# Half of four units' low parts on GpSimd, and fifteen top-k rounds of block 2 ahead of attention

## What is computed

```
def dsa_sparse_attention(h, pos, w_in, w_out):
    proj = h @ w_in                       # h is the normed x: rmsnorm(x, g)
    q, k, v, qi, ki, wi = jnp.split(proj, B_SPLITS, axis=-1)
    q, k, qi, ki = (partial_rope(t) for t in (q, k, qi, ki))
    def block(args):                      # 128 queries
        logits = jnp.einsum('bthd,bsd->bths', qi_blk, ki)
        score = jnp.einsum('bths,bth->bts', jax.nn.relu(logits), wi_blk)
        score = jnp.where(key_pos <= t, score, -jnp.inf)
        _, idx = lax.top_k(score, 128)
        s = einsum(q_blk, k[idx]) * HEAD_DIM ** -0.5
        pr = jax.nn.softmax(where(idx <= t, s, -inf))
        return einsum(pr, v[idx])
    return concat(blocks) @ w_out
```

## Time and profile before

| what | value |
|---|---|
| median of 3 runs | 1077.5 us (1077.49 to 1078.8) |
| profiled execution, its own time | 1078.13 us |
| its span | 1076.3 us, mean granted clock 0.997 |
| busy | TensorE 1056.6 us (98%), weight loads 859.0, VectorE 747.4 (69%), ScalarE 538.3 (50%), GpSimd 192.7 (18%) |
| DMA | 99.94 MB, mean 93 GB/s |

### The profile page before, as it was taken

One profiled execution on the slowest core, in us unless ns is written; L12 is line 12 of the kernel. 1 busy time (PEld: TensorE's weight loads), 2 busy tenths in 40 slices (PEclk: granted clock), 3 DMA queues, 4 the chain that ended last, 5 costly groups with the idle time before them and its releaser, 6 DMA issues.

```text
span 1076.3 us, 14866 instructions
## 1 busy us (share of the span) xinstructions
PE 1056.6 (98%) x5408; PEld 859.0 (80%) x5408; DVE 747.4 (69%) x1284; ACT 538.3 (50%) x1016; POOL 192.7 (18%) x335
## 2 busy tenths in 40 slices
PE   9999999999999999999999999999999999999997
PEld 8777779888888888888778766679888888888885
DVE  5455536586697697687579898526596696696684
ACT  6677545353453443425554567645254444453422
POOL 0465320000000000005403387520000000000005
PEclk9999999999999999999999999999999999999999
DMA  9531505645545445332623333006553535535502
GB/s 294 121 79 40 118 1 119 135 88 109 101 95 118 97 99 118 90 68 51 135 43 79 79 79 79 1 1 140 116 111 85 118 81 116 117 79 118 110 9 78
DMA packets 52009, 99.94 MB, mean 93 GB/s; under 512 B 4704, under 2 KB 4832, under 8 KB 51936
## 3 DMA queue, kind: packets, MB, share of 16 engines
q1 hardware_dynamic: 51216, 98.61, 40.9%
q10 hardware_dynamic: 720, 0.38, 0.1%
HBM read 96.88 MB, written 2.10 MB: 92 GB/s over the span
## 4 chain that ended last, share of the span: by engine, by line
PE 88%; DVE 5%; DMA 3%; ACT 1%; issue 1%; SPq 1%; POOL 0%; POOLq 0%; DVEq 0%; ACTq 0%
PE bank L2038 11%; PE bank L2039 11%; PE bank L2037 11%; PE bank L2397 7%; PE bank L2398 7%; PE bank L2396 7%; PE bank L2047 6%; PE bank L2049 5%; PE bank L2048 5%; PE bank L2186 3%; PE bank L2421 3%; PE bank L2420 3%; PE bank L2422 3%; PE bank L2255 2%; DMA w_raw<-in_a_w_in 2%; PE bank L2241 2%
## 5 line engine op out<-in xcount | busy, mean ns | idle before, releaser
L2037 PE MATMUL bank<-r_hi,w_hi 128*128 128x512 f32 (+1 forms) x456 | 177.5, 389 | 0.0
L2038 PE MATMUL bank<-r_hi,w_lo 128*128 128x512 f32 (+1 forms) x456 | 177.4, 389 | 0.0
L2039 PE MATMUL bank<-r_lo,w_hi 128*128 128x512 f32 (+1 forms) x456 | 177.4, 389 | 0.0
L1636 DVE TENSOR_TENSOR w_lo<-w_raw,w_hi 128x1024 fp32r<-128x1024 f32 x84 | 102.0, 1222 | 71.3 <-ACT w_hi L1165 71.2
L1165 ACT ACTIVATE w_hi<-w_raw 128x1024 fp32r<-128x1024 f32 x84 | 87.8, 1056 | 120.2 <-PE bank L2039 82.9
L2396 PE MATMUL bank<-w_hi,hid_hi 128*128 128x512 f32 x336 | 130.7, 389 | 0.0
L2397 PE MATMUL bank<-w_lo,hid_hi 128*128 128x512 f32 x336 | 130.7, 389 | 0.0
L2398 PE MATMUL bank<-w_hi,hid_lo 128*128 128x512 f32 x336 | 130.7, 389 | 0.0
L810 POOL TENSOR_TENSOR acc<-acc,G 128x512 f32<-128x512 f32 x8 | 13.0, 1650 | 594.3 <-ACT waste L1024 594.3
L1174 ACT ACTIVATE w_hi<-w_raw,gT 128x512 fp32r<-128x512 f32 x96 | 64.5, 715 | 106.0 <-DMA w_raw<-in_w_mlp_up 74.6
L2037 PEld LDWEIGHTS bank<-r_hi,w_hi 128*128 128x128 f32 (+1 forms) x456 | 85.2, 187 | 18.2
(11 more groups left out here) (213 smaller groups left out, 2149.4 us busy)
## 6 DMA issues: line engine op xcount, KB each, us to landing
w_raw<-in_w_mlp_up SPq DMA_DIRECT2D x64, 512.0 KB, 6.5
w_raw<-in_w_mlp_down SPq DMA_DIRECT2D x64, 512.0 KB, 7.0
w_raw<-in_b_w_in SPq DMA_DIRECT2D x16, 512.0 KB, 6.8
w_raw<-in_a_w_in SPq DMA_DIRECT2D x8, 512.0 KB, 9.1
w_raw<-in_a_w_out SPq DMA_DIRECT2D x8, 512.0 KB, 5.8
w_raw<-in_b_w_out SPq DMA_DIRECT2D x8, 512.0 KB, 6.0
xt<-in_x_turned SPq DMA_DIRECT2D x8, 256.0 KB, 5.7
X<-in_x SPq DMA_DIRECT2D x4, 512.0 KB, 11.2
```

What stands on the lines that cost most here:

```text
L1636: nc.vector.tensor_tensor(half_of(w_lo[:, u % 2, :], a), b_of(PRODUCTS[i][1], a), half_of(w_hi[:, u % 2, :], a).bitcast(f32), ALU.subtract ...
L2037: nc.tensor.matmul(bank, whi, xhi, start=start, stop=False)
L2038: nc.tensor.matmul(bank, wlo, xhi, start=False, stop=False)
L2039: return nc.tensor.matmul(bank, whi, xlo, start=False, stop=stop)
```

## The change

Units 56 to 59 (`RESCALED`) are treated in a new way. ScalarE makes the high parts of quarters 0 and 1 as before; then it multiplies quarters 2 and 3 of `w_raw` in place by their gains, and copies these without a scale as high parts. VectorE makes the low parts of quarters 0 and 1 alone. GpSimd makes those of quarters 2 and 3 by plain subtraction (`rest_low`), its pieces standing between the rotations. TensorE and SyncE wait for both (`low_of` and `rest_of`). VectorE does fifteen instead of eleven rounds of block 2 ahead of attention, in steps of three; the sixteenth and the final mask come behind turn 0, and turns 1 to 4 hold none of block 2 any more.

```diff
+RESCALED = (56, 57, 58, 59)
...
+        def rest_of(u):
+
+            return in_lo_done, 2 * RESCALED.index(u) + 2
...
             def load(u, src):
                 sp.wait_ge(*low_of(u - 2))
+                if u - 2 in RESCALED:
+                    sp.wait_ge(*rest_of(u - 2))
                 fetch(u, src)
...
+            def rest_low(u):
+
+                w_h, w_l = w_place(u)
+                whole = raw(RAW[u][0])
+                for k in (2, 3):
+                    cs = slice(512 * k, 512 * k + 512)
+                    pool.wait_ge(*((w_hi_part, part_hi_no(u, 2)) if k == 2 else (w_hi_done, hi_no(u))))
+                    nc.gpsimd.tensor_tensor(w_l[:, cs], whole[:, cs], w_h[:, cs].bitcast(f32), ALU.subtract).then_inc(in_lo_done, 1)
...
                     rope_q(10)
-                    for j in range(NB):
-                        rope_k(1, j)
-                    for qn in range(11, 17):
-                        rope_q(qn)
+                    rope_k(1, 0)
+                    rope_k(1, 1)
+                    rest_low(56)
+                    rope_k(1, 2)
+                    rope_k(1, 3)
+                    rest_low(57)
+                    rope_q(11)
+                    rope_q(12)
+                    rest_low(58)
+                    rope_q(13)
+                    rope_q(14)
+                    rest_low(59)
+                    rope_q(15)
+                    rope_q(16)
...
-                        last = nc.scalar.activation(w_h[:, cs], whole[:, cs], ACT.Copy,
-                                                    scale=gain(layer, 2 if name[:3] == "mlp" else 0, 4 * half_no(u) + k))
+                        if u in RESCALED and k == 2:
+                            for m in (2, 3):
+                                ms = slice(512 * m, 512 * m + 512)
+                                nc.scalar.activation(whole[:, ms], whole[:, ms], ACT.Copy,
+                                                     scale=gain(1, 0, 4 * half_no(u) + m)).then_inc(rescaled, 1)
+                        if u in RESCALED and k >= 2:
+                            act.wait_ge(rescaled, 2 * RESCALED.index(u) + k - 1)
+                            last = nc.scalar.activation(w_h[:, cs], whole[:, cs], ACT.Copy)
+                        else:
+                            last = nc.scalar.activation(w_h[:, cs], whole[:, cs], ACT.Copy,
+                                                        scale=gain(layer, 2 if name[:3] == "mlp" else 0, 4 * half_no(u) + k))
...
-            split(56)
+            split(56, (0, 1))
...
-            split(57)
+            split(57, (0, 1))
             k_low(1, 2)
             k_low(1, 3)
             top_rounds(1, TOPK // 8)
             top_mask(1)
-            top_rounds(2, 1)
+            top_rounds(2, 3)
             q_low(1, 11)
-            top_rounds(2, 4)
-            split(58)
+            top_rounds(2, 6)
+            split(58, (0, 1))
             q_low(1, 12)
-            top_rounds(2, 6)
-            split(59)
+            top_rounds(2, 9)
+            split(59, (0, 1))
             q_low(1, 13)
-            top_rounds(2, 8)
+            top_rounds(2, 12)
             q_low(1, 14)
-            top_rounds(2, 11)
-
-
-            ROUNDS_2 = (11, 12, 13, 14, 15, TOPK // 8)
+            top_rounds(2, 15)
+
+
+            ROUNDS_2 = (15, TOPK // 8)
...
                 if j == 0 and ks[0] == 0:
                     pe.wait_ge(*low_of(u))
+                    if u in RESCALED:
+                        pe.wait_ge(*rest_of(u))
```

More of the change, by code:

```diff
@@ L348, in hybrid_trunk @@
         w_in = [sem(f"w_in{n}") for n in range(5)]
-        w_hi_part = sem("w_hi_part")
+        w_hi_part, rescaled, in_lo_done = sem("w_hi_part"), sem("rescaled"), sem("in_lo_done")
         w_hi_done, w_lo_done, first_half_done = sem("w_hi_done"), sem("w_lo_done"), sem("first_half_done")
@@ L1413, in split @@
                                                               in1=w_h[:, cs].bitcast(f32), op0=ALU.mult, op1=ALU.subtract)
-                if ks[-1] == 3:
+                if ks[-1] == 3 or u in RESCALED:
                     last.then_inc(w_lo_done, 1)
```

## The result

The changed kernel takes 1080.53 us (median of 14 runs, 1078.89 to 1082.9), the kernel before, measured beside it, 1078.62 us (14 runs, 1077.31 to 1079.4). The ratio is 1.0023, with a 95% interval of 1.0015 to 1.003: **slower by 1.6 to 3.2 us**, 2.5 in the middle. The forecast was 1081.3 us and slower by 3.8. Of all executions in this document two took far longer than the rest, 3725 us (the units alone) and 2132 us (the kernel before); they are in no ratio, and their cause was not looked for.

A forecast was written before the change was run, and what follows sets the result against it. Only what makes TensorE wait was taken to change the time. Waits of 1.6 + 1.2 + 0.3 at units 57 to 59 and 0.7 of VectorE's remaining lateness made +3.8, so 1081.3 us; range 1078.2 to 1083.8.

The forecast's parts named there:

- The rival without turns: GpSimd's pieces run beside VectorE's as if alone; +1.0 us at the transposes of turn 2, 1078.5 us; chance 0.2.
- One of the forecast's signs: TensorE idle before the first matmuls of units 57 and 58, over 1 us each.
- The second slow stretch: TensorE's new waits bring a further stretch at the lower clock; +1.55 us, 1082.9 us; chance 0.22.
- The gates: First matmuls of units 57, 58 and 59, where TensorE waits for low parts; +1.6, +1.2 and +0.3 us.
- The arrivals at unit 57: VectorE reaches unit 57's low parts 0.8 us later than before, at 571.3.
- GpSimd's queue of rotations: Rotations of keys 2 and 3 and queries 13 to 16, queued behind GpSimd's pieces; costed at nothing.
- VectorE's sum: VectorE's lateness at query 15's low part and the first mask: 5.0 - 2.9 - 1.35 + 0.4 + 3.3 = +4.4 us.
- The absorption: VectorE's idle 1.00 us before the mask of turn 1 takes up 1.0 of its lateness: 4.4 to +3.4.
- the +3.8 at the transposes of turn 2: VectorE's lateness of 3.4 plus 0.4 for the final mask, reaching turn 2's transposes through its mask.
- The clock: From 619 to 623 us TensorE runs 3.4 us at the lower clock, costing 1.55 us.
- I keep one such stretch: One lower-clock stretch stays in the sum; none would be -1.55 us, a second one +1.55.
- Turns 1 to 4: Block 2's rounds taken out of these attention turns, 1.22 us each, lie behind turn 2's transposes; nothing won.

The follow-up runs named there:

- the units alone: The changed kernel with the rounds of block 2 where they were before; 1084.07 us, ratio 1.0053, and in a second run 1081.45 us, ratio 1.0024.
- the kernel with turn 0 free: The kernel before with turn 0's round of block 2 moved behind turn 5; 1077.01 us, ratio 0.9992, and once more 1076.28 us, ratio 0.9976.

## Why the prediction was right, and where it was off

**The direction and the mechanism** were right. TensorE waits at units 57, 58 and 59, because VectorE and GpSimd take turns there and, at unit 57, because of ScalarE's two more instructions. The rival without turns is refuted by the durations (2.45 and 3.32 together, 1.42 and 2.55 apart). One of the forecast's signs failed: TensorE was to idle over 1 us before unit 58 as well, and idled 0.78. The second slow stretch did not appear in the changed kernel's two traces. It did in the one with the units alone: two stretches, from 576.36 and from 637.80.

**The gates.** Unit 57: +1.6 forecast, 1.69 measured. Unit 58: +1.2 forecast, 0.85 measured. Unit 59: +0.3 forecast, 0.49 measured. Sum: 3.1 forecast, 3.03 measured. The arrivals at unit 57 were right too: VectorE 0.76 us later than before (0.8 forecast). The forecast took ScalarE's two more instructions into the sum beside the turns, and the run without the rescaling shows that both were needed: with the turns alone the wait at 57 was half as long. What GpSimd's queue of rotations cost was not tested.

**VectorE's sum was mis-sized:** "Three of the four remaining quarters are held for about 1.1 each: +3.3". Only one quarter of each unit was held: the other started before GpSimd's first piece, by 0.26 us at unit 58, and kept its 0.75 us; the pairs of 2.45 us (unit 58) and 2.46 us (unit 59) show it. Two in place of three are 2 x 1.03 = 2.1 us, and the sum is +3.2 in place of +4.4; the mask of turn 0 was 3.30 us late. The absorption was mis-sized with it. VectorE still idled 0.73 us before the mask of turn 1 in place of 1.00, so 0.27 was absorbed and not 1.0: TensorE, whose scores it waits for, was just as late. The two errors nearly cancel, and the +3.8 at the transposes of turn 2 came out as 3.44 and 3.69.

**The clock** was the larger error in the sum: "I keep one such stretch". The stretch is no constant of the kernel. Half of the changed kernel's runs (7 of 14) have a mean granted clock of 0.998, as has the profiled execution without a stretch, and average 1080.15 us; the other half lie at 0.994 to 0.997 and average 1081.3. Of the 74 runs of the kernel before that stood beside the experiments, none is above 0.997. In the two traces of the changed kernel the next X comes 1.36 us later than in the first trace of before without a stretch and 3.14 with one. What a stretch costs is not constant either: by the next X 1.78 us between the changed kernel's two traces, 0.75 for the second 3.4 us in the kernel before (194.57 and 195.32), 0.23 in the kernel with turn 0 free. So what it takes off the forecast's 3.8 is only an estimate: half of the 1.15 us between the two halves of the runs, 0.6 us, or half of 1.6, 0.8 us. Another 0.1 to 0.4 was missing at turn 2 already. The rest of the distance to the measured 2.5 was not tested on its own.

**Turns 1 to 4** were costed at nothing won for block 2's rounds taken out of them, and the traces show nothing won: the next wait of scores for a mask, near 653 us, is 1.10 and 0.70 us in the two traces of before, 0.72 and 0.86 in the two of the changed kernel. The point stood one turn earlier. Both kernels do a round in turn 0, right ahead of the mask on which turn 2's 1.69 us hang. That wait, the longest of the span, was named as the bound, and the change left the round in its place and added a mask. The runs that take it away gain 1.0 us at this wait in both kernels, of which later waits take back a part.

## What to carry to other kernels

Sharing a split between VectorE and GpSimd did not pay where both read two operands from SBUF at the same time. Check first whether a pair of instructions takes as long together as one after the other, and then whether the receiver can start before the giver's share is due, counting every step ahead of its input. Two chains of nearly equal lateness hide each other's parts: undoing one part gives little (0.6 to 1.2 of 3.4 us at the mask of turn 2 here), and costs found alone don't add. Where one wait is the longest of the span, look first at the single piece of movable work right ahead of what it waits for before moving anything larger: it was worth 0.9 and 2.6 us in two measurements here, where the large change lost 2.5.

## What the runs showed of the hardware that was not expected

The lower clock comes and goes between executions of one and the same program: none, 3.4 or 6.8 us at 1.2 GHz near turn 2, and in some executions 3.4 us behind unit 57's wait of 1.88 us (from 576.36 and 576.60), but not behind the same wait in three others. The same wait was followed by such a stretch in one execution and not in the next.

VectorE and GpSimd take turns by whole instructions when both read two fp32 operands from SBUF, and who starts first is not slowed. In the changed kernel, at units 57, 58 and 59, VectorE's first quarter keeps its 0.75 us; then GpSimd's piece ends 1.13 to 1.16 us behind VectorE's and VectorE's quarter 0.54 to 0.55 behind GpSimd's. Where GpSimd starts first (unit 57 without the rescaling), its piece keeps 1.30 us and VectorE's small instruction goes from 0.29 to 1.14. A held instruction ends sooner behind the other's end than its own duration (1.15 for 1.28, 0.55 for 0.75), so a turn is somewhat cheaper than the two durations in a row. The Trainium skill (SBUF — State Buffer, Who interferes with whom) states of VectorE's two-port modes that whoever issues first gets the shared pair for the whole instruction and the other fully blocks, and of a VectorE instruction with two inputs from SBUF that it contends with a GpSimd instruction that reads SBUF. These traces agree with the second statement and show that the first describes such two-input instructions as well.
